# Reordering the closing stage of a hybrid convolution decoder layer: gate, embedding, projection

## What is computed

```python
m = jax.nn.sigmoid(gate_a) * ya + jax.nn.sigmoid(gate_b) * yb
h = h + jnp.einsum('ntd,de->nte', m, w_o)
pe = jnp.einsum('ntp,pd->ntd', p.astype(h.dtype), w_pe)
pg = jax.nn.sigmoid(jnp.einsum('ntd,de->nte', _rmsnorm(h, g_ple), w_pg))
h = h + pg * pe
y = _rmsnorm(h, g_final)
```

## Time and profile before

| what | value |
|---|---|
| median of 3 timed runs | 909.31 us (854.02 to 979.31) |
| profiled execution, its own time | 848.59 us |
| its span, first to last instruction, slowest core | 846.7 us |
| spans of all cores | 839.6 to 846.7 us |
| TensorE busy | 805.5 us, 95% |
| VectorE, ScalarE, GpSimd busy | 466.4, 315.6, 213.9 us |

### The profile page before, as it was taken

The page is one execution under the profiler, slowest core; times in us unless marked ns, Lnnn a source line. Parts: engine busy times, 40 slices in busy tenths (PEclk is TensorE's granted clock), DMA queues, the critical chain, the costliest instruction groups (busy, mean ns, idle before and its releaser), DMA issues.

```text
span 846.7 us, 15797 instructions; the slowest of 8 cores (839.6 to 846.7 us)
## 1 busy us (share of the span) xinstructions
PE 805.5 (95%) x5896; PEld 405.8 (48%) x5988; DVE 466.4 (55%) x473; ACT 315.6 (37%) x428; POOL 213.9 (25%) x362
## 2 busy tenths in 40 slices
PE   3999999999999999899999999999999999999995
PEld 2844444444444444344455555555545555554442
DVE  3535655557295222468545566667756932323566
ACT  4233333343254412466333322233433633113554
POOL 3211122211133211243243342234211321000322
PEclk9999999999999999999999999999999999999998
DMA  8598899995899996889799766788445999012533
GB/s 232 85 152 160 147 138 174 171 171 79 139 145 166 202 163 120 180 218 231 174 167 166 116 127 120 125 151 138 70 88 83 142 171 197 15 42 74 149 100 124
DMA packets 114891, 118.75 MB, mean 140 GB/s; under 512 B 71392, under 2 KB 74720, under 8 KB 113760
## 3 DMA queue, kind: packets, MB, share of 16 engines
q0 software_dynamic: 33776, 61.19, 47.8%
q1 hardware_dynamic: 80896, 56.28, 26.8%
q10 hardware_dynamic: 144, 0.26, 0.1%
HBM read 147.95 MB, written 15.74 MB: 193 GB/s over the span
## 4 chain that ended last, share of the span: by engine, by line
PE 80%; DVE 6%; DMA 6%; issue 4%; SPq 2%; ACT 1%; POOL 1%; DVEq 0%; POOLq 0%; ACTq 0%
PE ps L537 63%; PE ps L967 7%; PE ps L1037 5%; DMA t_c<-x 1%; PE ps L1024 1%; DVE t_tmp L893 1%; SPq L879 1%; PE ps L680 1%; DVE t_c L912 1%; PE ps L1132 1%; DMA vd<-t_xv 1%; DMA t_xv<-x 1%; DMA t_acc<-t_tmp 1%; DMA t_wr<-vd 1%; PE ps L1121 1%
## 5 line engine op out<-in xcount | busy, mean ns | idle before, releaser
L537 PE MATMUL ps<-t_uT,t_ring 128*128 128x512 bf16 (+1 forms) x2747 | 516.8, 345 | 7.7 <-issue 4.6
L537 PEld LDWEIGHTS ps<-t_uT,t_ring 128*128 128x128 bf16 x2816 | 251.5, 98 | 266.8 <-issue 1.4
L368 POOL DMA_DIRECT2D t_ring<-w_in x144 | 77.9, 542 | 337.1 <-PE ps L537 289.4
L921 ACT ACTIVATE t_tmp<-ps 128x1024 f32<-128x1024 f32 (+1 forms) x32 | 34.4, 1075 | 129.6 <-PE ps L537 129.6
L967 PE MATMUL ps<-t_wr,t_c 128*128 128x512 bf16 x268 | 62.9, 387 | 2.6 <-DVE t_tmp L1063 2.4
L926 DVE SCALAR_TENSOR_TENSOR t_tmp<-t_tmp,ps 128x1024 f32<-128x1024 f32 (+1 forms) x16 | 20.6, 1288 | 80.7 <-PE ps L537 80.7
L537 PE MATMUL ps<-t_c,t_ring 128*128 128x512 bf16 (+1 forms) x316 | 61.4, 347 | 1.1 <-DVE t_c L912 0.9
L537 PE MATMUL ps<-t_ya,t_ring 128*128 128x512 bf16 (+1 forms) x314 | 61.0, 346 | 0.4 <-issue 0.2
L1037 PE MATMUL ps<-t_wr,t_ta 128*128 128x512 bf16 x265 | 60.6, 379 | 0.8 <-DMA t_ta<-t_acc 0.2
L814 DVE SCALAR_TENSOR_TENSOR t_tmp<-t_xv,t_vecs,t_tmp 128x1024 f32<-128x1024 f32 (+1 forms) x48 | 46.7, 973 | 5.0
L611 DVE SCALAR_TENSOR_TENSOR t_xv<-t_tmp,ps 128x1024 bf16<-128x1024 f32 x14 | 17.1, 1222 | 55.1 <-PE ps L537 55.1
(11 more groups left out here) (110 smaller groups left out, 784.3 us busy)
## 6 DMA issues: line engine op xcount, KB each, us to landing
t_ring<-w_in POOLq DMA_DIRECT2D x144, 256.0 KB, 5.8
t_xv<-x SPq DMA_DIRECT2D x26, 512.0 KB, 6.3
y<-t_tmp SPq DMA_DIRECT2D x16, 512.0 KB, 3.1
vd<-t_xv SPq DMA_DIRECT2D x16, 264.0 KB, 6.0
t_wr<-vd SPq DMA_DIRECT2D x32, 132.0 KB, 6.3
t_wr<-t_wr SPq DMA_DIRECT2D x16, 263.9 KB, 4.5
t_wr<-t_wr SPq DMA_DIRECT2D x16, 263.9 KB, 5.3
t_c<-x SPq DMA_DIRECT2D x8, 512.0 KB, 14.0
```

The source lines that it names most:

```text
L368: S.add("pool", lambda e, k=k, src=src: e.dma_start(out=ring[k][:, :], in_=src), reads=[f"wu{g}"] if g >= 0 and gate else [], writes=[f"ri ...
L537: S.add("pe", lambda e: e.matmul(psf[:, 512 * b + lo:512 * b + hi], lhsT=ring[k_][:, 128 * k:128 * k + 128], rhs=src[:, k, lo:hi], start=( ...
L921: S.add("act", lambda e: e.activation(out=tg[:, 0:T], in_=pf(bg_), func=AF.Tanh, scale=0.5), reads=pres(bg_), writes=[tgr])
```

## The change

In each round the projection of tile t+2 now stands behind the embedding product on TensorE. `B_sq(t)` and `D_out(t)` run in the tile's own round, no longer one later. On VectorE E1(t), E2(t) and n_turn(t+2) stand ahead of A_stt(t+2), except in round 0; on ScalarE the squares of x and B_sq(t) stand ahead of A_xb(t+2). In the last block's last tile the embedding product is cut in halves too and follows the gate's halves; the first half is multiplied by gfin early, on VectorE, and scaled at the end on ScalarE, while VectorE scales the second.

```diff
             def pe_last():
+                held["pe"] = palloc()
                 held["pg"] = palloc()
-                pe_mm(nt - 1)
+                if not last:
+                    pe_mm(nt - 1)
...
-                for k, h in order:
+                for i, (k, h) in enumerate(order):
+                    if halves and i == NCH:
+                        pe_mm(t, 0)
...
+                if halves:
+                    pe_mm(t, 1)
...
                 G_tanh(t)
-                if t + 2 == nt:
-                    A_turn_pe(t + 1)
-                    A_turn_copy(t + 1)
-                if t > 0 and t + 2 < nt:
-                    A_mm(t + 2)
-                if t > 0 and t + 1 < nt:
-                    pe_mm(t)
-                if t + 2 == nt:
-                    pe_last()
-                if t > 0:
-                    B_sq(t - 1)
+                ahead = t + 2 < nt
                 more = t + 2 < len(nxt)
-                if more:
-                    n_stats(t + 2)
-                if t + 2 < nt:
+
+                def A_vec():
                     A_stt(t + 2)
                     A_xb(t + 2)
                     if t + 3 < nt:
                         A_turn_dma(t + 2)
                     xgo()
+                if t + 2 == nt:
+                    A_turn_pe(t + 1)
+                    A_turn_copy(t + 1)
+                if t > 0 and t + 1 < nt:
+                    pe_mm(t)
+                if t + 2 == nt:
+                    pe_last()
+                if t > 0 and ahead:
+                    A_mm(t + 2)
+                if more:
+                    n_stats(t + 2)
+                if t == 0:
+                    A_vec()
                 E1(t)
                 E2(t)
-                if t + 2 < nt:
-                    A_sq(t + 2)
                 if more:
                     n_turn(t + 2)
-                if t > 0:
-                    D_out(t - 1)
+                if ahead or not last:
+                    B_sq(t)
+                if t > 0 and ahead:
+                    A_vec()
+                if ahead:
+                    A_sq(t + 2)
+                if ahead or not last:
+                    D_out(t)
                 xgo()
...
                 B_sq(t - 1)
+                S.add("dve", lambda e: e.tensor_tensor(out=yt[:, 0:512], in0=B[:, 0:512], in1=gfin[:, 0:512], op=ALU.mult),
+                      reads=[f"B{sl}_0", "gfin"], writes=[f"yt{yl}_0"])
...
-                s6["r3", t] = rs_of(cs)
-                D_out(t, 0, "sp")
-                D_out(t, 1, "act")
-            else:
-                B_sq(t)
-                D_out(t)
+                s6["r3", t] = ap, res = rs_of(cs)
+                S.add("act", lambda e: e.activation(out=yt[:, 0:512], in_=yt[:, 0:512], func=AF.Copy, scale=ap),
+                      reads=[f"yt{yl}_0", res], writes=[f"yt{yl}_0"])
+                D_out(t, 1, "sp")
+                S.add("act", lambda e: e.dma_start(out=y_d[tiles[t]:tiles[t] + 128, 0:512], in_=yt[:, 0:512]),
+                      reads=[f"yt{yl}_0"], dma="yth0", out=True)
```

More of the change, by code:

```diff
@@ L1014, in pe_last, with pe_mm @@
             def pe_last():
+                held["pe"] = palloc()
                 held["pg"] = palloc()
-                pe_mm(nt - 1)
+                if not last:
+                    pe_mm(nt - 1)
             held = {}
-            def pe_mm(t):
-                b = palloc()
+            def pe_mm(t, only=None):
+                b = held["pe"] if t == nt - 1 else palloc()
                 for q in range(2):
-                    for h in range(2):
+                    for h in range(2) if only is None else (only,):
                         S.add("pe", lambda e, h=h, q=q: e.matmul(
@@ L1350, in do_block @@
             if last:
-                sl = t % 3
-                cs = []
+                sl, yl = t % 3, t % 2
+                B, yt, cs = Bbuf[sl], ybuf[yl], []
                 G_tanh(t, 0)
@@ L1360, in do_block @@
                 for h in range(2):
-                    cs.append(sq_sum(Bbuf[sl][:, 512 * h:512 * h + 512], [f"B{sl}_{h}"], 512))
+                    cs.append(sq_sum(B[:, 512 * h:512 * h + 512], [f"B{sl}_{h}"], 512))
                 D_out(t - 1)
-                s6["r3", t] = rs_of(cs)
-                D_out(t, 0, "sp")
-                D_out(t, 1, "act")
-            else:
-                B_sq(t)
-                D_out(t)
+                s6["r3", t] = ap, res = rs_of(cs)
[4 more added lines that the diff above has]
+                      reads=[f"yt{yl}_0"], dma="yth0", out=True)
         for bi, blk in enumerate(BLOCKS):
```

## The result

| | median of 12 runs, us | lowest |
|---|---|---|
| before | 854.0 | 849.82 |
| changed | 858.28 | 854.38 |

The ratio is 1.0058, with a 95% interval of 1.0035 to 1.0081. The medians are of all runs; the ratio leaves out those in which one half of the chip ran at a lower clock (4 of 12 before, 3 of 12 changed). The change makes the kernel slower, by less than two per cent: 4.9 us by this ratio. A second comparison, made later, gave 858.24 against 848.06: 1.0103 (1.0073 to 1.0132), or 8.7 us. By the two intervals the loss is between 3 and 11 us.

The account below looks back on a forecast made before the run. Two places were to decide: the tail, and whether the new order still feeds TensorE in the rounds. From 848.59 us, + 5.8 (first block) + 0.1 (last block) - 1.9 (tail) gave 852.6, range 845.5 to 862.

Parts of the forecast that it names:

- The level: Starting time of the sum: the profiled execution's 848.59 us, taken as undisturbed; timed runs' 5.4 above it left to the range.
- the first block's loss: First block's closing stage: the seam to the last block opens at 416.4 against 410.64, 5.8 us lost.
- the tail's gain: End of the program: second half's work earlier and final scalings side by side, 1.9 us gained.
- The ring: First block's rounds: a new chain from tanh through VectorE and ScalarE to the next tanh, 8.85 us against TensorE's 7.8.
- The hold of GpSimd's power under E2: First block's rounds: GpSimd's power cannot pass E2, so n_turn starts at about 4.3 instead of 3.68, 0.62 us.
- TensorE's waits: First block: TensorE waits some 1.1 us at each gate from round 3 on, about 2.2 before tile 7's transposes.
- E1: Tail, on VectorE: this instruction's second half starts at 837.85 instead of 839.17, 1.3 us earlier.
- The last block: Its rounds: no n_turn, so the ring is 7.0 us, under 7.8; cost 0.1 us (0 to 1.0).
- The lock misses: Rival, first block: the power gets ahead of E2 at no cost, ring 8.21 to 8.25, 849.4 us; chance 0.16.
- no ring: Rival: ScalarE and VectorE keep up in the rounds, the seam's 0.73 goes, the tail pays, 845.7 us; chance 0.18.
- The clock falls: Rival: waits at gates and tile 7's transposes lower TensorE's clock, 1.7 us each, 856.9 us, up to 859; chance 0.20.

Follow-up runs that it names:

- x_stats_early: The changed kernel with the squares of x and their statistics ahead of the round's tanh, from round 1 of the first block: 860.68 us, 1.0147 to before.
- stt_then_turn: The changed kernel with n_turn(t+2) moved behind A_stt(t+2) in the first block: 850.61 us, 1.0037 to before.
- tail_only: The kernel before with only the last tile in the new form and the old rounds: 851.66 us, 1.0027 to before.
- no_store7: The changed kernel without the y store of the last block's tile 7: tail 8.13 us on the median core, 8.15 with the store.
- round0_later: The changed kernel with B_sq(0) and D_out(0) at the end of round 1, first block only: 853.52 us, 1.0066 to before.
- best: old_first_seam with the PSUM pairs taken in before's order in the first block: 848.77 us, 1.0004 to before.
- best_again: The kernel best measured a second time, nothing changed: 849.84 us, 0.9996 to before.
- old_first_seam: The changed kernel with before's order in the first block, but the ninth x tile's statistics ahead of the squares in round 6: 851.26 us, 1.0019 to before.

## Why the prediction was wrong

The prediction had 852.6 us, 4.0 above the profiled 848.59. Two things must be kept apart: the level, and the difference, which was 4.9 us by the ratio of the first comparison, 8.7 by that of the second and 7.3 by the pieces. Two steps failed. The level was taken from one profile, and in the sum the first block's loss (5.8, measured 8.0) was too small and the tail's gain (1.9, measured 1.2) too large.

**The level.** "The profiled one is the undisturbed level" failed. The median of before was 854.0 us, above its profiled 848.59 by the 5.4 that the prediction named and left to the range. Against that median the forecast of 852.6 is a gain of 1.4 us, while its own sum, and the measurement, are a loss. In the later comparisons before's median was 848.06 to 850.77, near the profiled one; the level of one profile is no better known than that.

**The ring (the mechanism, right).** The links summed to 8.85 us (8.21 + 0.62 is 8.83); measured 8.84 to 9.00 on every core, twice. The hold of GpSimd's power under E2 was predicted from the earlier trace rows, measured at 1.59 us, and x_stats_early took it out for 0.6 us a round. stt_then_turn took n_turn and the hold out and left 7.1, where the links without it sum to 7.0. From A_stt(2) to the seam the working has 416.4 - 356.92 = 59.5 us; measured 60.1 to 60.2 on the eight cores of two executions on which the seam's product waited. This was not luck: the links, the hold and the order were each seen in the trace or taken out by a run.

**The first block's loss (+ 5.8; measured + 8.0).** This is the term that was mis-sized. Its own chain was 0.6 us short (59.5 for 60.1). The larger part is the other side of the subtraction: the 5.8 was taken against core 0, whose x tile came late, and which had the gap of 2.38 us and the slow clock behind it in this very stage. From A_stt(2) to the seam it took 53.7 us there and 52.8 on the median core of before, 0.9 less. Measured the same way the changed kernel needs 7.3 more than the median core. The last 0.7 came up between the seam and the piece's other end, and 0.46 of it is the clock behind tile 7's transposes (see the rivals).

**TensorE's waits.** "Some 1.1 us at each gate from round 3 on": core 4 has 1.04, 0.79 and 0.67 behind its first wait of 3.07, core 7 has 0.40 and 0.71. The one not foreseen is the first, 2.71 to 3.07 us on six cores, at the gate of tile 3, the first at which TensorE's lead is used up; on cores 3 and 5 it is spread over more gates. The releaser is the turned tile, as predicted. "About 2.2 before tile 7's transposes": 2.17 to 2.36 on all cores.

**The tail (- 1.9; measured - 1.2).** Each step up to the last issue was right: 1.2 from E1 (1.3 predicted), the last issue at 5.02 (5.0 predicted). The rest is lost in the transfers behind it, at which the prediction did not look: from the last issue to the end of the span it is 3.1 us (8.15 - 5.06), where it was 2.4 (9.37 - 7.0). Issued 0.04 us apart the two halves land after 2.6 to 3.0 us, where 0.67 apart they took 2.0 to 2.4. That the closer issue is the cause is argued, not shown. tail_only shows besides that the gain hangs on D_out's new round.

**The last block (+ 0.1; measured + 0.4 to 0.6).** The last tile's embedding product now stands in its gate, so tile 7's four matmuls alone cover the copy ahead of that gate, and TensorE pauses 0.2 us there. The rest is a wait for a turned tile in a middle round, 0.2 us in core 7's bracket and 0.4 in core 0's.

**The rivals.** "The lock misses" and "no ring" fell with the spacing. "The clock falls" came in part, in both places that it named, and cost less than it said.
- At the gate of tile 3 the clock fell on four of the six cores that waited 2.7 us or more, and again on four of six the second time (4.9 to 5.3 us for sixteen matmuls). It cost nothing that can be seen, for the ring and not TensorE led: without a fall at the transposes, cores with and without this one need 65.1 to 65.2 us from A_stt(2) to the piece's end.
- Behind the wait ahead of tile 7's transposes it fell on 8 of 16 cores (2.9 to 3.6 us for the eight embedding matmuls, not 1.89). These cores need 65.6 us, 0.46 more, where the rival had 1.7. Those without the fall wait 0.8 to 0.9 us at the seam, those with it do not: part of the delay takes the place of that wait. no_store7 and round0_later show the same step of 0.46.

What stays open: why a ninth x tile made ready earlier lengthens VectorE's lag behind TensorE 200 us on (the runs show that it does, not by which instruction), why the clock falls on some cores and not on others behind the same wait, and how much of the slowest core's time comes from its late arrival at the closing stage.

## What to carry to other kernels

Before an instruction is moved to its own round, write down the chain that comes back to the same instruction one round later, and compare its length with the leading engine's round. Two engines that both have idle time can form a ring longer than the loaded engine's round, and an instruction put into their idle time lengthens the ring if it stands between two links (the squares of x: + 1.04 us a round).

Take a difference on the same typical core on both sides: the slowest core is picked for its bad luck, and its late tile or slow clock may stand in the very stage that is compared. Count it from an event behind what varies: from A_stt(0) on round0_later looked 0.35 us shorter, from A_stt(2) on it was 1.5. And look for what a gain at one place meets later: here 0.8 us at the seam was given back 200 us on, by a longer wait and the clock behind it.

## What the runs showed of the hardware

- A wait does not decide alone whether TensorE's clock falls. In the two executions of the changed kernel gate waits of 2.5 to 3.1 us lowered it on 8 of 12 cores, and the waits of 1.7 to 2.4 ahead of the transposes on 8 of 16 (2.26 and 2.27 us were among those that did not). At line 857 a pair of waits of 1.4 to 1.5 and 0.62 us, with two short matmuls between, lowered it on 10 of 32 cores (five in best, two in best_again, three in x_stats_early, none in old_first_seam); with 1.0 to 1.2 and 0.62 it fell on 2 of the 80 cores of the other ten traces. Core 5 of best then ran at 0.72 of full over four us, between the levels of 1.2 and 2.4 GHz; a fall there cost 1.4 to 2.7 us in best. The Trainium skill ("TensorE: Matmul & The Clock Gate", section "HAM oscillation") warns of recurring waits in a loop; in this case the ring's other gate waits, 0.2 to 1.9 us round after round, brought no fall, and single longer waits and a single pair of waits did.
- What a fall costs depends on who leads: nothing in the ring (65.1 to 65.2 us with and without it), 0.46 us ahead of the seam, where part of it replaces another wait, and 1.4 to 2.7 at line 857, where TensorE leads.
- A GpSimd instruction on 128 numbers that starts 0.04 us behind a VectorE one of 128x1024 takes 1.59 us instead of 0.55, and the next VectorE instruction, which needs its result, waits 0.5 for it.
- Two output transfers of 256 KB issued 0.04 us apart landed after 2.6 to 3.0 us, against 2.0 to 2.4 when they were issued 0.67 us apart.
